# Tail of a mixture-of-experts layer: how the expert rows are read back, summed and finished

## The chip, the cores and the metric

The kernel runs on one core of one Trainium2 chip. The metric is device time in microseconds (us): the median of several executions. Beside them stands one profiled execution, whose trace is what is read below; it has its own time and its own span (first to last instruction). Engines: PE is TensorE, DVE is VectorE, ACT is ScalarE, POOL is GpSimd, SP is SyncE, which here only starts transfers and waits. A letter q behind an engine's name means its instruction queue: it waits or issues a transfer while the engine itself stays idle.

## The reference

One layer of a streaming encoder for 256 prompt tokens and 64 sample tokens of width 1024: attention of two kinds, then a mixture of experts. What the change touches is only the last line of the layer, the sum of a token's two chosen experts, its gate, and the residual:

```python
    top_w, top_i = lax.top_k(pe, TOP_K)                      # TOP_K = 2
    top_w = top_w / jnp.sum(top_w, axis=-1, keepdims=True) * pg_sel
    gate = jnp.sum(jax.nn.one_hot(eid, N_EXPERTS, dtype=jnp.float32) * top_w[..., None], axis=1)
    hid = jax.nn.silu(jnp.einsum('nd,edf->nef', hf, w1)) * jnp.einsum('nd,edf->nef', hf, w3)
    hid = hid * gate[..., None].astype(hid.dtype)
    y = jnp.einsum('nef,efd->nd', hid, w2)
    ...
    x = x + g2 * _hier_moe(h2, w_rg, b_rg, w_re, b_re, w1, w3, w2)
```

All values are fp32.

## The kernel before

Tokens lie on the 128 partitions in three tiles: tile 0 and tile 1 are the prompt (128 rows each), tile 2 is the sample (64 rows, `rows_of(2)`). Each engine has its own hand-written instruction stream; semaphores order them. Most of the time goes to attention and projections, and then to the expert loop: 16 pairs of experts, whose weights (`ew`, `e_w` in the trace) SP loads in 1 MB transfers. For each pair POOL gathers token rows, PE runs the two up projections (`hidden`) and the down projection (`down`, line 999, called through the helper `mm`, line 550), ACT and DVE bring the result into `y_sb`, weighted with the token's gate, and POOL scatters the rows with an indirect DMA (line 1881) to `y_dram` (`expert_rows` in the trace) in the chip's main memory. A token's two experts give two rows there, one in each half of the tensor, `TOK` rows apart.

After the loop comes the tail, which the change rewrites. All waits here are in program order on each engine:

- POOL waits until the last scatter has landed (`y_stored`, line 1901), and then issues six loads (line 1905), in the order tile 0, tile 2, tile 1, each time `ya` (first half of `y_dram`) and `yb` (second half). A load of a prompt tile is 512 KB, of the sample 256 KB. Each tile has its semaphore, `back[t]`, complete at 32.
- DVE takes the prompt tiles: wait for `back[t]`, `ya + yb` (line 1749), times the gate `g2b` (line 1751), plus the residual `x_sb` (line 1753), 128x1024 each, with a drain between.
- POOL takes the sample tile with the same three operations at 64x1024 (lines 1908, 1910, 1912), and then raises `y_sample_done`.
- SP stores tile 0 and tile 1 (line 530) as DVE finishes them (`y_done`), and then the sample (line 532) after `y_sample_done`; then it waits for all stores and the program ends.
- PE and ACT have nothing to do in the tail. PE's last work is a slot table (`slot_table`, names `EV` and `R`), made at the end of each round of the expert loop.

Of the kernel before, what the change touches and what calls it, by code (L numbers as in the profile page):

```python
# [7 lines left out]
P = 128  # L8
D = 1024
KD = D // P  # L10
SEQ, DEC, PAST = 256, 64, 256
TOK = SEQ + DEC
TILES = 3
# [18 lines left out]
ALU = mybir.AluOpType  # L32
# [43 lines left out]
def rows_of(t):  # L76
    return P if t < 2 else DEC


def build(nc, t_in, t_out):  # L80
    g = t_in
    ctx = ExitStack()
    with ctx:
        def sem(name):
            return ctx.enter_context(nc.semaphore(name))
# [5 lines left out]
        def place(name, shape, dt, at):  # L91
            assert at + 4 * int(np.prod(shape[1:])) <= end, name
            return nc.alloc_sbuf_tensor_at(name, shape, dt, offset=at)
# [3 lines left out]
        def take(name, shape, dt=F32):  # L97
            at = cursor[0]
            cursor[0] += (4 * int(np.prod(shape[1:])) + 31) // 32 * 32
            return place(name, shape, dt, at)  # L100

        cst = take("cst", [P, C_ALL])
        ident = cst[:, C_ID:C_ID + P]
# [28 lines left out]
        x_sb = take("x_sb", [P, TILES, D])  # L132
# [79 lines left out]
        ya, yb = (place(n, [P, TILES, D], F32, ew_at + 2 * 4 * (2 * KD * FE + 2 * D) * (j + 1)) for j, n in enumerate(("ya", "yb")))  # L212
        cursor[0] = hT_at
        g2b = take("g2b", [P, 2, D])
# [53 lines left out]
        ps = ctx.enter_context(nc.psum_tensor("ps", [P, 8, 512], F32))  # L268
# [3 lines left out]
        y_dram = nc.dram_tensor("expert_rows", [1 + 2 * TOK, D], F32).ap()  # L272
# [39 lines left out]
        g2_in = sem("g2_in")  # L312
        o_done = sem("o_done"); o_added = sem("o_added")
# [11 lines left out]
        e_y = sem("e_y"); e_ya = sem("e_ya"); e_yv = sem("e_yv")  # L325
        y_stored = [sem(f"y_stored{j}") for j in range(2)]
        back = [sem(f"back{t}") for t in range(TILES)]
        y_done = sem("y_done"); y_sample_done = sem("y_sample_done"); stored = sem("stored")


        ADA_BANK = 1
# [18 lines left out]
        def _(sp):  # L350
# [171 lines left out]
            with sp.Fori(0, count) as r:  # L522
# [2 lines left out]

                sp.wait_ge(rounds_ready, 1)
                sp.reg_load(count, rnd_i[0:1, 0:1])
            for t in range(2):
                sp.wait_ge(y_done, t + 1)
                sp.dma_start(t_out["y_prompt"][t * P:(t + 1) * P], x_sb[:, t, :]).then_inc(stored, 16)  # L530
            sp.wait_ge(y_sample_done, 1)
            sp.dma_start(t_out["y_sample"], x_sb[0:DEC, 2, :]).then_inc(stored, 16)
            sp.wait_ge(stored, 48)
            for s in a_stored + b_stored:
# [4 lines left out]
        def _(pe):  # L539
# [381 lines left out]
            def slot_table(r):  # L921

                for n in range(2):
                    built = pe.to_reg(2 * r + n + 1)
                    pe.wait_ge(r_rows, 1)
                    pe.wait_ge(r_slot, built)
                    for t in range(TILES):
                        rows = rows_of(t)
                        last = mm(ps[:, 7, 0:3 * EXPERTS], R[0:rows, 3 * n + t, :],
                                  EV[0:rows, 3 * n + t, :, :].rearrange("p a e -> p (a e)"), n == 0 and t == 0)  # L930
                    pe.free_register(built)
                last.then_inc(tab_out, 1)
# [72 lines left out]
            with pe.Fori(0, rounds) as r:  # L1005
# [8 lines left out]
                down(r, PAIRS - 1)  # L1014
                slot_table(r + 1)


        @block.scalar
        def _(act):
# [265 lines left out]
            def columns_out(r, p):  # L1285

                act.wait_ge(e_Ta, PAIRS * r + p + 1)
                act.wait_ge(e_h, PAIRS * r + p + 1)
                A(xgT[p % 2][:, 0:4, :], ps[:, 0, :].rearrange("p (k s) -> p k s", k=4), ACT.Copy).then_inc(e_xTa, 1)

            def expo(r, p):

                act.wait_ge(e_h, PAIRS * r + p + 3)
                act.wait_ge(e_hid, PAIRS * r + p + 1)
                A(h_e[p % 2][:], ps[:, 2 + p % 2, 0:FE], ACT.Exp, scale=-1.0).then_inc(e_exp, 1)  # L1295

            def hid_out(r, p):

                act.wait_ge(e_hT, PAIRS * r + p + 3)
                act.wait_ge(e_y, PAIRS * r + p + 1)  # L1300
                A(hidT[p % 2][:], ps[:, 4, 0:2 * P].rearrange("p (m s) -> p m s", m=2), ACT.Copy).then_inc(e_hTc, 1)  # L1301

            def rows_out(r, p):

                act.wait_ge(e_y, PAIRS * r + p + 3)
                act.wait_ge(y_stored[p % 2], 16 * (8 * r + p // 2 + 1))
                A(y_sb[p % 2][:, 0:512], ps[:, 5, :], ACT.Copy, scale=row_w[:, p:p + 1]).then_inc(e_ya, 1)

            with act.Fori(0, rounds) as r:
                act.wait_ge(tab_ready, r + 1)  # L1310
                columns_out(r, 0)
                for p in range(PAIRS):
                    expo(r, p)
                    if p + 1 < PAIRS:
                        columns_out(r, p + 1)
                    if p:
                        rows_out(r, p - 1)
                    hid_out(r, p)
                rows_out(r, PAIRS - 1)


        @block.vector
        def _(dve):
            V = nc.vector
# [76 lines left out]
            for k in range(KD):  # L1401
                last = V.tensor_scalar(h_sample[:, k, :], xnT[:, k, SEQ:TOK], gain1[:, k, 1:2], mod[:, k, 1:2], ALU.mult, ALU.add)
# [187 lines left out]
            for u in range(4):  # L1590
                for t in range(TILES):
                    n, r = 3 * u + t, rows_of(t)
# [56 lines left out]
            for n, eh in enumerate((eh1, eh2)):  # L1649
                dst = E1[:, n].rearrange("p t (g e) -> p t g e", g=GROUPS)  # L1650
# [71 lines left out]
            with dve.Fori(0, rounds) as r:  # L1722
# [3 lines left out]
                for half in range(2):  # L1726
                    c = slice(SLOTS * half, SLOTS * (half + 1))
                    own = ps[c, 7, 0:3 * EXPERTS].rearrange("s (a p two) -> s a p two", a=3, two=2)[:, :, :, half]
                    V.tensor_scalar(idx[c], own[:, 0:2, :], float(NO_ROW), None, ALU.add)
                    last = V.tensor_copy(row_w[c, :], own[:, 2, :])  # L1730
# [13 lines left out]


            dve.wait_ge(g2_in, 16)
            for t in range(2):
                dve.wait_ge(back[t], 32)
                V.tensor_tensor(ya[:, t, :], ya[:, t, :], yb[:, t, :], ALU.add)
                dve.drain()  # L1750
                V.tensor_tensor(ya[:, t, :], ya[:, t, :], g2b[:, 0, :], ALU.mult)
                dve.drain()
                V.tensor_tensor(x_sb[:, t, :], x_sb[:, t, :], ya[:, t, :], ALU.add).then_inc(y_done, 1)


        @block.gpsimd
        def _(pool):
            G = nc.gpsimd
# [91 lines left out]
            for n in range(2):  # L1850
                src = late_cst[:, L_ROW + 6 * n:L_ROW + 6 * n + 6].rearrange("p (t a) -> p t a", a=2)
                last = G.tensor_tensor(EV[:, 3 * n:3 * n + 3, 0:2, :], E1[:, n].unsqueeze(2).broadcast_to([P, TILES, 2, EXPERTS]),
                                       src.unsqueeze(3).broadcast_to([P, TILES, 2, EXPERTS]), ALU.mult)
# [45 lines left out]
            pool.wait_ge(setup_done, 1)  # L1899
            for j in range(2):  # L1900
                pool.wait_ge(y_stored[j], stored_rows)
            for t in (0, 2, 1):
                for n, dst in enumerate((ya, yb)):
                    first, r = 1 + n * TOK + t * P, rows_of(t)
                    pool.dma_start(dst[0:r, t, :], y_dram[first:first + r]).then_inc(back[t], 16)
            pool.wait_ge(back[2], 32)
            pool.wait_ge(g2_in, 16)
            G.tensor_tensor(ya[0:DEC, 2, :], ya[0:DEC, 2, :], yb[0:DEC, 2, :], ALU.add)
            pool.drain()
            G.tensor_tensor(ya[0:DEC, 2, :], ya[0:DEC, 2, :], g2b[0:DEC, 1, :], ALU.mult)  # L1910
            pool.drain()
            G.tensor_tensor(x_sb[0:DEC, 2, :], x_sb[0:DEC, 2, :], ya[0:DEC, 2, :], ALU.add).then_inc(y_sample_done, 1)


_SHAPES = (("y_prompt", (1, SEQ, D)), ("y_sample", (1, DEC, D)),
# [26 lines left out]
```

## Time and profile before

| | us |
|---|---|
| median of 3 runs | 851.24 (851.11 to 852.28) |
| the profiled execution, its time | 850.77 |
| the profiled execution, its span | 849.0 |
| PE busy in that span | 714.0 (84%) |
| DVE busy | 349.2 (41%) |
| POOL busy | 102.9 (12%) |

The profiled execution's time is 1.77 us longer than its span: what lies around the first and last instruction. It lies 0.47 us under the median. The profile gives shares over the whole span; the change is in its last 24 us, so what matters is read from that stretch: the chain of work that ended last, the timeline of each engine there, and the load of the DMA engines in short stretches. "Idle before" in a group of instructions names what ended the engine's wait. The column PEclk gives the TensorE clock that was granted in a stretch, as a part of 2.4 GHz; 0.50 is 1.2 GHz, and there are only these two levels.

### The profile page before, as it was taken

Reading aid. Unit: us, or ns where it says so; the run is one execution under the profiler, and the core shown is the slowest. Engines: PE = TensorE matmul, PEld = TensorE weight load, DVE = VectorE, ACT = ScalarE, POOL = GpSimd, SP = SyncE. Lnnn points to the kernel's source line nnn. Section 1 sums busy time; section 2 is a strip of 40 time slices with the busy share of each in tenths; the row PEclk is TensorE's granted clock in tenths of the full one; section 3 lists DMA queues with packets and bytes.
Section 4 is the critical chain, followed back from the end, with each engine's and each line's share of the span. In section 5 each row is a group of like instructions: output and inputs, shape, how many; then the busy total and the mean of one; then the engine's idle time right before and its main releaser. Section 6 shows DMA issues by size and latency. Waiting matters only on the chain.

```text
span 849.0 us, 13795 instructions
## 1 busy us (share of the span) xinstructions
PE 714.0 (84%) x5329; PEld 585.2 (69%) x5329; DVE 349.2 (41%) x548; ACT 271.0 (32%) x499; POOL 102.9 (12%) x161
## 2 busy tenths in 40 slices
PE   0797999999899799999988999638997887888770
PEld 0386888887699799999978999525554644644540
DVE  1556666776343243334423455531323123113123
ACT  1445455554443334455334531300111011001000
POOL 2012222222000001000100000010011001001014
PEclk9899999999899899999999999857999989989895
DMA  9947277765636576542215342699799999999705
GB/s 323 326 137 225 70 210 219 217 196 181 199 101 187 148 224 178 135 114 77 80 49 178 101 148 100 252 422 416 320 416 417 418 419 417 419 416 418 313 17 182
DMA packets 131176, 199.17 MB, mean 235 GB/s; under 512 B 11688, under 2 KB 113464, under 8 KB 117816
## 3 DMA queue, kind: packets, MB, share of 16 engines
q1 hardware_dynamic: 123032, 185.63, 61.7%
q0 software_dynamic: 6208, 11.02, 3.7%
q10 hardware_dynamic: 1888, 1.86, 0.7%
q8 instruction: 32, 0.52, 0.3%
q14 instruction: 16, 0.13, 0.0%
HBM read 193.47 MB, written 16.55 MB: 247 GB/s over the span
## 4 chain that ended last, share of the span: by engine, by line
PE 63%; issue 20%; ACT 6%; DVE 4%; POOL 2%; POOLq 2%; ACTq 1%; DVEq 1%; DMA 0%
PE ps L550 35%; PE ps L545 8%; PE ps L547 7%; PE ps L546 7%; ACT w_hi L1066 3%; DVE w_lo L1378 1%; PE ps L945 1%; PE ps L949 1%; PE ps L981 1%; PE ps L713 1%; ACT sig_r L1183 1%; DVEq L1587 1%; ACT z_na L1228 1%; PE ps L696 0%; POOLq L1777 0%
## 5 line engine op out<-in xcount | busy, mean ns | idle before, releaser
L550 PE MATMUL ps<-e_w,xgT 128*64 128x256 f32 x1024 | 129.7, 417 | 32.6 <-issue 31.3
L550 PEld LDWEIGHTS ps<-e_w,xgT 128*64 128x64 f32 x1024 | 91.2, 151 | 66.8 <-issue 40.2
L545 PE MATMUL ps<-hT_hi,w_hi 128*128 128x320 f32 x320 | 102.6, 321 | 5.5 <-DVE w_lo L1378 5.2
L1378 DVE TENSOR_TENSOR w_lo<-raw,w_hi 128x2048 fp32r<-128x2048 f32 (+1 forms) x27 | 71.5, 2647 | 83.9 <-ACT w_hi L1066 83.9
L546 PE MATMUL ps<-hT_lo,w_hi 128*128 128x320 f32 x320 | 99.9, 312 | 0.0
L547 PE MATMUL ps<-hT_hi,w_lo 128*128 128x320 f32 x320 | 99.8, 312 | 0.0
L1707 DVE TENSOR_SCALAR h_s<-h_e 128x256 f32<-128x256 f32 x16 | 4.7, 294 | 162.8 <-ACT h_e L1295 162.8
L1066 ACT ACTIVATE w_hi<-raw 128x2048 fp32r<-128x2048 f32 (+1 forms) x27 | 59.1, 2190 | 28.3 <-PE ps L547 28.3
L545 PEld LDWEIGHTS ps<-hT_hi,w_hi 128*128 128x128 f32 x320 | 61.0, 191 | 7.9 <-DVE w_lo L1378 5.5
L546 PEld LDWEIGHTS ps<-hT_lo,w_hi 128*128 128x128 f32 x320 | 61.2, 191 | 0.0
L547 PEld LDWEIGHTS ps<-hT_hi,w_lo 128*128 128x128 f32 x320 | 61.1, 191 | 0.0
L550 PE MATMUL ps<-e_w,hidT 128*64 128x512 f32 x256 | 58.4, 598 | 0.6 <-ACT hidT L1301 0.6
L1295 ACT ACTIVATE h_e<-ps 128x256 f32<-128x256 f32 x16 | 6.2, 384 | 153.5 <-PE ps L550 153.5
L545 PE MATMUL ps<-w_hi,hT_hi 128*128 128x384 f32 x128 | 45.3, 354 | 0.0
L546 PE MATMUL ps<-w_lo,hT_hi 128*128 128x384 f32 x128 | 43.5, 340 | 0.0
L547 PE MATMUL ps<-w_hi,hT_lo 128*128 128x384 f32 x128 | 43.4, 339 | 0.0
L1881 POOL DMA_INDIRECT expert_rows<-y_sb,idx x16 | 16.2, 1012 | 215.4 <-DVE y_sb L1720 189.5
L545 PE MATMUL ps<-oT_hi,w_hi 128*128 128x320 f32 x128 | 40.5, 316 | 1.1 <-DVE oT_lo L1545 1.1
L546 PE MATMUL ps<-oT_lo,w_hi 128*128 128x320 f32 x128 | 40.2, 314 | 0.0
L547 PE MATMUL ps<-oT_hi,w_lo 128*128 128x320 f32 x128 | 40.2, 314 | 0.0
L550 PEld LDWEIGHTS ps<-e_w,hidT 128*64 128x64 f32 x256 | 17.5, 136 | 29.6 <-issue 27.8
L550 PE MATMUL ps<-ada_late,c_cols 128*32 128x128 f32 x512 | 32.7, 283 | 0.0
(261 smaller groups left out, 1283.8 us busy)
## 6 DMA issues: line engine op xcount, KB each, us to landing
e_w<-in_w SPq DMA_DIRECT2D x96, 1024.0 KB, 23.3
raw<-in_w_in SPq DMA_DIRECT2D x45, 512.0 KB
ada_late<-in_w_ada SPq DMA_DIRECT2D x16, 1024.0 KB, 5.1
ada_first<-in_w_ada SPq DMA_DIRECT2D x8, 1024.0 KB, 21.7
raw<-in_w_in SPq DMA_DIRECT2D x8, 1024.0 KB
raw<-in_w_oa SPq DMA_DIRECT2D x4, 1024.0 KB
raw<-in_w_ob SPq DMA_DIRECT2D x4, 1024.0 KB
raw<-in_w_out SPq DMA_DIRECT2D x4, 1024.0 KB
```

The costliest lines, as they stand in the source:

```text
L545: nc.tensor.matmul(out, lhs_hi, rhs_hi, start=first, stop=False, skip_group_check=True)
L546: nc.tensor.matmul(out, lhs_hi, rhs_lo, start=False, stop=False, skip_group_check=True)
L547: return nc.tensor.matmul(out, lhs_lo, rhs_hi, start=False, stop=last, skip_group_check=True)
L550: return nc.tensor.matmul(out, lhs, rhs, start=first, stop=last, skip_group_check=True)
L713: last = nc.tensor.transpose(ps[:, b, c * P:(c + 1) * P], amap[:, n * P:(n + 1) * P], ident)
L945: last = nc.tensor.transpose(ps[:, 0, k * P:(k + 1) * P], xg[p % RING][:, k:D:KD], ident)
L949: last = nc.tensor.transpose(ps[:, 1, (k - 4) * P:(k - 3) * P], xg[p % RING][:, k:D:KD], ident)
L981: last = nc.tensor.transpose(ps[:, 4, m * P:(m + 1) * P], hid[j][:, m:FE:2], ident)
L1066: A(w_hi[j][:, :, 0:width], raw[j][:, :, 0:width], ACT.Copy).then_inc(split_hi, 1)
L1183: A(sig_r[m][:], sig[m][:], ACT.Ln, bias=1.0)
L1378: V.tensor_tensor(w_lo[j][:, :, 0:width], raw[j][:, :, 0:width], f32(w_hi[j][:, :, 0:width]), ALU.subtract).then_inc(split_done, 1)
L1881: G.indirect_dma_start(y_dram, bass.IndirectOffsetOnAxis(ap=idx[:, 1, p:p + 1], axis=0), y_sb[j][:], None, bounds_check=2 * TOK, oob_is_er ...
```

## The change

Three things change, all behind the expert loop.

1. Loads. POOL, when the last scatter has landed, raises a new semaphore `scattered`. SP then loads both rows of tile 0, ACT both rows of tile 1, POOL itself both rows of tile 2. The six transfers and their bytes are the same.
2. Sum. For each tile in the order 0, 1, 2 PE waits for `back[t]` and adds the two rows: for each half of 512 columns one matmul with the identity as the stationary operand and `ya` as the moving one, and one with `yb` that accumulates on it, into PSUM banks `2t` and `2t + 1`. That is 4 fp32 matmuls of 512 columns a tile, 12 in all.
3. Finish. DVE finishes all three tiles with two operations each: PSUM times `g2b` into `ya`, and `x_sb + ya`. POOL's three operations on the sample are gone. SP stores tile 0 and the sample, ACT stores tile 1.

```diff
+            sp.wait_ge(scattered, 1)
+            for n, dst in enumerate((ya, yb)):
+                sp.dma_start(dst[:, 0, :], y_dram[1 + n * TOK:1 + n * TOK + P]).then_inc(back[0], 16)
+            sp.wait_ge(y_done, 1)
+            sp.dma_start(t_out["y_prompt"][0:P], x_sb[:, 0, :]).then_inc(stored, 16)
+            sp.wait_ge(y_done, 3)
             sp.dma_start(t_out["y_sample"], x_sb[0:DEC, 2, :]).then_inc(stored, 16)
...
+            for t in range(TILES):
+                rows = rows_of(t)
+                pe.wait_ge(back[t], 32)
+                for half in range(2):
+                    c = slice(half * 512, (half + 1) * 512)
+                    mm(ps[0:rows, 2 * t + half, :], ident[0:rows, 0:rows], ya[0:rows, t, c], True, False)
+                    last = mm(ps[0:rows, 2 * t + half, :], ident[0:rows, 0:rows], yb[0:rows, t, c], False)
+                last.then_inc(o_done, 1)
...
+            act.wait_ge(scattered, 1)
+            for n, dst in enumerate((ya, yb)):
+                act.dma_start(dst[:, 1, :], y_dram[1 + n * TOK + P:1 + n * TOK + 2 * P]).then_inc(back[1], 16)
+            act.wait_ge(y_done, 2)
+            act.dma_start(t_out["y_prompt"][P:2 * P], x_sb[:, 1, :]).then_inc(stored, 16)
...
-            for t in range(2):
-                dve.wait_ge(back[t], 32)
-                V.tensor_tensor(ya[:, t, :], ya[:, t, :], yb[:, t, :], ALU.add)
+            for t in range(TILES):
+                rows = rows_of(t)
+                dve.wait_ge(o_done, 13 + t)
+                V.tensor_tensor(ya[0:rows, t, :].rearrange("p (b c) -> p b c", b=2), ps[0:rows, 2 * t:2 * t + 2, :],
+                                g2b[0:rows, t // 2, :].rearrange("p (b c) -> p b c", b=2), ALU.mult)
                 dve.drain()
-                V.tensor_tensor(ya[:, t, :], ya[:, t, :], g2b[:, 0, :], ALU.mult)
-                dve.drain()
-                V.tensor_tensor(x_sb[:, t, :], x_sb[:, t, :], ya[:, t, :], ALU.add).then_inc(y_done, 1)
+                V.tensor_tensor(x_sb[0:rows, t, :], x_sb[0:rows, t, :], ya[0:rows, t, :], ALU.add).then_inc(y_done, 1)
...
-            for t in (0, 2, 1):
-                for n, dst in enumerate((ya, yb)):
-                    first, r = 1 + n * TOK + t * P, rows_of(t)
-                    pool.dma_start(dst[0:r, t, :], y_dram[first:first + r]).then_inc(back[t], 16)
-            pool.wait_ge(back[2], 32)
-            pool.wait_ge(g2_in, 16)
-            G.tensor_tensor(ya[0:DEC, 2, :], ya[0:DEC, 2, :], yb[0:DEC, 2, :], ALU.add)
...
+            pool.nop().then_inc(scattered, 1)
+            for n, dst in enumerate((ya, yb)):
+                first = 1 + n * TOK + 2 * P
+                pool.dma_start(dst[0:DEC, 2, :], y_dram[first:first + DEC]).then_inc(back[2], 16)
```

On POOL, behind the last scatter, these rows stand in the kernel before (`ya` and `yb` are the two row buffers, a row with 64x1024 is the sample's; in brackets the semaphores that an instruction waits for):

```order
L1905 DMA ya<-expert_rows 128x1024 [waits y_stored1,y_stored0,setup_done]
L1905 DMA yb<-expert_rows 128x1024
L1905 DMA ya<-expert_rows 64x1024
L1905 DMA yb<-expert_rows 64x1024
L1905 DMA ya<-expert_rows 128x1024
L1905 DMA yb<-expert_rows 128x1024
L1908 TENSOR_TENSOR ya<-ya,yb 64x1024 [waits g2_in,back2]
L1910 TENSOR_TENSOR ya<-ya,g2b 64x1024
L1912 TENSOR_TENSOR x_sb<-x_sb,ya 64x1024
```

and these in the changed one, from the last scatter to the end:

```order
L1898 DMA expert_rows<-y_sb_180,idx 641x1024 [waits e_yv,y_stored0,e_ya,setup_done]
L1903 REGISTER_ALU
L1903 COMPARE_AND_BRANCH
L1915 ISA
L1922 DMA ya<-expert_rows 64x1024 [waits y_stored1,setup_done,y_stored0]
L1922 DMA yb<-expert_rows 64x1024
```

Four of POOL's six loads have moved to SP and ACT, and its three operations are gone.

On PE the program before ends with the slot table of the round behind the last:

```order
L924 ISA
L550 MATMUL ps<-EV,R 128x96 [waits r_slot,r_rows]
L550 MATMUL ps<-EV,R 128x96 x2
L924 REGISTER_ALU
L550 MATMUL ps<-EV,R 128x96 [waits r_slot,r_rows]
L550 MATMUL ps<-EV,R 128x96 x2
L1005 REGISTER_ALU
L1005 COMPARE_AND_BRANCH
```

In the changed one the sums stand behind the loop's branch (`cst` holds the identity). The rows of tile 1 follow those of tile 0 in the same form, the sample's with 64x512:

```order
L552 MATMUL ps<-EV,R 128x96 x2
L1007 REGISTER_ALU
L1007 COMPARE_AND_BRANCH
L552 MATMUL ps<-ya,cst 128x512 [waits back0]
L552 MATMUL ps<-yb,cst 128x512
L552 MATMUL ps<-ya,cst 128x512
L552 MATMUL ps<-yb,cst 128x512
L552 MATMUL ps<-ya,cst 128x512 [waits back1]
```

PE now stands between the loads and DVE, tile after tile.

## Rows read from the trace of the kernel before

**Rows 1.** Page, chain that ended last: shares of the span by engine.
```profile
PE 63%; issue 20%; ACT 6%; DVE 4%; POOL 2%; POOLq 2%; ACTq 1%; DVEq 1%; DMA 0%
```

**Rows 2.** Chain in order of time, its end: start us, us, what.
```profile
822.78 2.72 DMA expert_rows<-y_sb,idx
...
826.07 0.58 POOL ya L1905
...
829.33 4.84 issue
834.16 3.15 POOLq L1909
837.31 3.26 issue
840.57 2.62 POOLq L1911
...
843.32 2.36 POOLq L83
```

**Rows 3.** Timeline of the tail: start us, us, engine, line, operation, idle before.
```profile
831.29 1.23 DVE L1749 TENSOR_TENSOR ya<-ya,yb 128x1024 f32<-128x1024 f32 x1 [8.26 <-DMA yb<-expert_rows]
832.60 1.23 DVE L1751 TENSOR_TENSOR ya<-ya,g2b 128x1024 f32<-128x1024 f32 x1
...
835.15 6.22 SPq L530 DMA_DIRECT2D out_y_prompt<-x_sb  x2
836.68 1.72 DVE L1749 TENSOR_TENSOR ya<-ya,yb 128x1024 f32<-128x1024 f32 x1 [1.55 <-DMA yb<-expert_rows]
...
845.71 0.52 SPq L532 DMA_DIRECT2D out_y_sample<-x_sb  x1
```

**Rows 4.** Half-microsecond stretches: busy us by engine, then PEclk, DMA share, GB/s.
```profile
825.00:825.50 0.50, 0.00 (x0) 0.00 (x0) 0.00 (x0) 0.00 (x0) 0.00 (x0) 0.50 0.05 8
827.00:827.50 0.50, 0.00 (x0) 0.00 (x0) 0.00 (x0) 0.00 (x0) 0.50 (x2) 0.50 0.53 74
828.00:828.50 0.50, 0.00 (x0) 0.00 (x0) 0.00 (x0) 0.00 (x0) 0.50 (x2) 0.50 1.04 319
830.00:830.50 0.50, 0.00 (x0) 0.00 (x0) 0.00 (x0) 0.00 (x0) 0.00 (x0) 0.50 0.96 393
...
832.50:833.00 0.50, 0.00 (x0) 0.00 (x0) 0.42 (x2) 0.00 (x0) 0.00 (x0) 0.50 1.13 221
...
835.00:835.50 0.50, 0.00 (x0) 0.00 (x0) 0.12 (x1) 0.00 (x0) 0.50 (x1) 0.50 1.09 434
835.50:836.00 0.50, 0.00 (x0) 0.00 (x0) 0.00 (x0) 0.00 (x0) 0.50 (x1) 0.50 0.20 74
```

**Rows 5.** The scatters of line 1881, sixteen of 512 KB: issue to landing.
```profile
DMA to landing us min/median/max: 2.6/8.1/9.2
```

**Rows 6.** Page, DMA issues: the weight loads that run beside them.
```profile
e_w<-in_w SPq DMA_DIRECT2D x96, 1024.0 KB, 23.3
```

**Rows 7.** Timeline of the last down projection; DVE reads PSUM before and behind it.
```profile
815.29 0.42 DVE L1711 TENSOR_TENSOR h_s<-h_s,ps 128x256 f32<-128x256 f32 x1
...
817.41 3.65 PE L550 MATMUL ps<-e_w,hidT 128*64 128x512 f32 x16 [0.63 <-ACT hidT L1301]
...
821.10 0.75 DVE L1720 TENSOR_SCALAR y_sb<-ps,row_w 128x512 f32<-128x512 f32 x1 [4.14 <-PE ps L550]
```

**Rows 8.** Timeline of PE in attention: an fp32 matmul on the whole array.
```profile
315.82 0.86 PE L550 MATMUL ps<-z_sp,cst 128*128 128x384 f32 x2
316.52 0.38 PE L550 MATMUL ps<-z_sp,ones_neg 128*128 128x128 f32 x2
```

**Rows 9.** Stretches behind a restart of PE: columns as in the stretches above.
```profile
689.23:694.98 5.75, 5.75 (x28) 3.66 (x30) 0.00 (x0) 0.00 (x0) 0.00 (x0) 0.50 1.01 417
...
803.83:807.62 3.79, 3.79 (x20) 2.74 (x22) 0.00 (x0) 0.00 (x0) 0.00 (x0) 0.55 0.28 109
807.62:811.41 3.79, 3.79 (x38) 3.02 (x37) 0.00 (x0) 0.00 (x0) 0.00 (x0) 1.00 0.02 8
```

More of the change, by code:

```diff
@@ L327, in build @@
         back = [sem(f"back{t}") for t in range(TILES)]
-        y_done = sem("y_done"); y_sample_done = sem("y_sample_done"); stored = sem("stored")
+        y_done = sem("y_done"); scattered = sem("scattered"); stored = sem("stored")
         ADA_BANK = 1
@@ L527, in _ @@
                 sp.reg_load(count, rnd_i[0:1, 0:1])
-            for t in range(2):
-                sp.wait_ge(y_done, t + 1)
-                sp.dma_start(t_out["y_prompt"][t * P:(t + 1) * P], x_sb[:, t, :]).then_inc(stored, 16)
-            sp.wait_ge(y_sample_done, 1)
+            sp.wait_ge(scattered, 1)
[4 more added lines that the diff above has]
+            sp.wait_ge(y_done, 3)
             sp.dma_start(t_out["y_sample"], x_sb[0:DEC, 2, :]).then_inc(stored, 16)
@@ L1746, in _ @@
             dve.wait_ge(g2_in, 16)
-            for t in range(2):
-                dve.wait_ge(back[t], 32)
-                V.tensor_tensor(ya[:, t, :], ya[:, t, :], yb[:, t, :], ALU.add)
+            for t in range(TILES):
[3 more added lines that the diff above has]
+                                g2b[0:rows, t // 2, :].rearrange("p (b c) -> p b c", b=2), ALU.mult)
                 dve.drain()
-                V.tensor_tensor(ya[:, t, :], ya[:, t, :], g2b[:, 0, :], ALU.mult)
-                dve.drain()
-                V.tensor_tensor(x_sb[:, t, :], x_sb[:, t, :], ya[:, t, :], ALU.add).then_inc(y_done, 1)
+                V.tensor_tensor(x_sb[0:rows, t, :], x_sb[0:rows, t, :], ya[0:rows, t, :], ALU.add).then_inc(y_done, 1)
         @block.gpsimd
@@ L1901, in _ @@
                 pool.wait_ge(y_stored[j], stored_rows)
-            for t in (0, 2, 1):
-                for n, dst in enumerate((ya, yb)):
-                    first, r = 1 + n * TOK + t * P, rows_of(t)
-                    pool.dma_start(dst[0:r, t, :], y_dram[first:first + r]).then_inc(back[t], 16)
-            pool.wait_ge(back[2], 32)
-            pool.wait_ge(g2_in, 16)
-            G.tensor_tensor(ya[0:DEC, 2, :], ya[0:DEC, 2, :], yb[0:DEC, 2, :], ALU.add)
[L1909 to L1912, printed above, removed]
+            pool.nop().then_inc(scattered, 1)
+            for n, dst in enumerate((ya, yb)):
+                first = 1 + n * TOK + 2 * P
+                pool.dma_start(dst[0:DEC, 2, :], y_dram[first:first + DEC]).then_inc(back[2], 16)
 _SHAPES = (("y_prompt", (1, SEQ, D)), ("y_sample", (1, DEC, D)),
```

## The prediction

> **What bounds the kernel now.** First the page's chain that ended last: PE holds 63% of it [rows 1], so over the whole span the matmuls are the bound. The change touches none of that; it lies in the last 24 us, and there the chain looks different. Read it in order of time [rows 2]: the last scatter, issued at 822.78, lands 2.72 us later, at 825.50; POOL begins to issue its six loads at 826.07 and is through at 829.33; then it waits 4.84 us for the sample's rows; and from 834.16 on the chain is POOL's own three operations, 3.15, 2.62 and 2.36 us, with a hole of 3.26 us between the first two. They end at 845.68, and SP stores the sample at 845.71 [rows 3]. The span ends at 849.0, so this store and the end of the program take 3.3 us. DVE is not on that path: it has the rows of tile 0 at 831.29 and of tile 1 at 836.68 [rows 3].
>
> The second view is the load of the DMA engines [rows 4]. Packets of the six loads run from about 827.1 to 835.5. They fill the engines from 828.0 on (share near 1.0), at 319 to 434 GB/s for prompt tiles and only 221 GB/s while the 64-row sample is moved. So the loads are bound by the DMA engines, not by their issue, except for the first microsecond.
>
> The third view is the column PEclk: PE has stopped before 825 and its clock stands at 0.50, which is 1.2 GHz, through the whole tail [rows 4].
>
> So now the path is: scatter landed (825.5), sample's rows there (834.2), POOL's 11.5 us, store 3.3 us.
>
> **The change, part by part.**
>
> *POOL's sample work goes.* 834.16 to 845.68, 11.5 us, leaves the path. What is late next is PE, which must sum three tiles, and DVE behind it.
>
> *The loads start on three queues.* SP and ACT need no software issue of 0.55 us each. SP's store issued at 835.15 [rows 3] had packets before 836.0 [rows 4], at most 0.85 us later; POOL's first load took about 1.0 us (826.07 to 827.1), and POOL waited 0.57 us behind the landing before that. With SP released at about 825.65, packets begin at 826.5, 0.6 us earlier than now. When does tile 0 land, call it T0? Earliest: SP's tile is served alone, as POOL's first is now: 831.29 - 0.6 = 830.7. Latest: all share evenly and end as the last load does now: 836.68 - 0.6 = 836.1. Between them: SP's and ACT's tiles together are 2.1 MB, 5.2 us at some 400 GB/s, from 826.5 to 831.7, and landing is seen about 0.8 us behind the last packet (830.5 and 831.29 for tile 0): 832.5. The sample takes up to 2.4 us of the engines in between (half a megabyte at 221 GB/s): 834.9. I take the middle, T0 = 833.7, because queues share here and none goes first: scatters that POOL issued beside a weight queue 23.3 us deep [rows 6] landed after 8.1 us in the median and 2.6 at best [rows 5]. They neither waited for that queue nor passed it.
>
> The Trainium skill, page "DMA: Bandwidth & Descriptors", section "Issuing engines are not separate DMA queues", speaks against this part: transfers from scalar, sync or gpsimd run on the same 16 DMA engines and interleave, and several issuers save only the issue time. By that rule, too, this part gains the 0.6 us alone; if instead each queue had its own bandwidth, T0 would be near 830.7. The full DMA share behind a single queue agrees with the rule [rows 4]; no row here shows two hardware queues side by side.
>
> *PE's 12 matmuls.* An fp32 matmul shows as two records, that is two passes: the last down projection has 8 in its code and 16 in the trace [rows 7]. Those work in two halves of the array side by side (128*64), so each half passes 8 times 512 columns in 3.65 us, 0.456 us a pass. Nearest check on the whole array: two passes of 384 columns before the next instruction starts, 315.82 to 316.52, 0.70 us [rows 8], which scales to 0.47 for 512 columns. A tile here is 4 matmuls, 8 passes: 3.65 us at full clock, the sample too, since its columns count and not its 64 rows. Three tiles: 10.9 us (11.2 by the second row). Lower bound: if the halves were not side by side, a pass would be 3.65/16 = 0.228 us, and three tiles 5.5 us.
>
> *The clock.* PE starts at half clock after 9 us of idling. Behind seven waits of 3 to 4 us in the expert loop the full clock came back 3.8 to 5.75 us after PE's restart; the longest and the shortest stand in [rows 9], with 0.50 and 0.55 granted until then. 20 records fitted in 3.79 us, and 38 in the next 3.79 us at 1.00. Half of such a stretch is lost: 1.9 to 2.9 us. I take 2.3. Upper bound: the clock never rises, then the whole 10.9 us come once more.
>
> *DVE.* Two operations a tile instead of three. The second is an SBUF add like those of 1.23 us; the first reads PSUM. 0.42 us for 256 columns and 0.75 for 512 [rows 7] bound it between 1.23 and 1.5 us. With the pitch of 1.31 us between two operations (831.29 to 832.60), 1.31 + 1.23 = 2.6 us a tile with the handover (DVE's 821.10 follows PE's end at 821.06). That is less than PE's 3.65, so tiles 0 and 1 hide under PE's next tile, and only the sample's 2.6 us are on the path. If PE were twice as fast this cover would go, and DVE's 3 x 2.6 would be the bound (below).
>
> *What costs nothing.* The nop for `scattered` is POOL's and SP, ACT and POOL wait anyway; SP and ACT have nothing queued behind their waits but the stores. The stores of tiles 0 and 1 leave while PE works on later tiles. Only the sample's store stays, at 3.3 us as now.
>
> *Sum.* 833.7 + 10.9 + 2.3 + 2.6 + 3.3 = 852.8, against a span of 849.0: **3.8 us longer**. POOL's 11.5 us are replaced by 10.9 + 2.3 + 2.6 = 15.8, and the start is 0.5 us earlier. The profiled execution took 850.77 with its 1.77 us around the span, so it would be 854.6; it lies 0.47 under the median of 851.24, so the median becomes 855.0. With all lower bounds of this case (T0 832.5, clock 1.9) it is 853.4, with the upper ones (T0 836.1, passes 11.2, clock 2.9, DVE 0.3 more) 858.6.
>
> **The rivals.**
>
> *SP first.* Tile 0 lands at 830.7, and PE sums it while the others arrive. The rest is as above, as tile 1 is there by 836.1, before PE asks for it at half clock. 3.0 us less: span 849.8, median 852.0, no measurable change. For it: SP issues first by a hair. Against it: the sharing in rows 5. Chance 0.12.
>
> *Cheap passes* (the other side). If a pass of 512 columns costs 0.228 us, tile 0 is summed at half clock in 3.65 us and then DVE is the bound, three times 2.6: T0 + 3.65 + 7.8 + 3.3. That is 848.5 with T0 = 833.7 (median 850.7, no change) and 845.5 with 830.7 (median 847.7, faster). It decides where T0 lies under 832.5. Against it: 0.70 us for two passes of 384 columns on the whole array [rows 8]. The same holds if the identity matmul were done in one pass. Chance 0.06, faster 0.04 and unchanged 0.02 of it.
>
> *Cold to the end.* The clock stays at 0.50 for all 12 matmuls: 10.9 us in place of 2.3, span 861.4, median 863.6. Against it: in the expert loop it came back within 5.75 us of steady work [rows 9]. The Trainium skill, page "TensorE: Matmul & The Clock Gate", section "HAM oscillation — how this bites in real kernels", warns of small bursts between waits for DMA that run throttled; the granted 0.50 behind earlier waits agrees. It would decide if PE had to wait between tiles, and it does not, if they land together. Chance 0.06.
>
> **How the numbers follow.** My forecast, 855.0, has 0.72; SP first 0.12, cheap passes 0.06, cold 0.06; 0.04 is left for something slower that I don't see. A measurement of this kernel tells about 0.2% from no change, 1.7 us: under 849.5 is faster, over 852.9 slower. So faster 0.04, same 0.15 (SP first, cheap passes, and 0.01 of the forecast's own edge), slower 0.81. The range runs from 851.6, which takes in SP first, to 858.6, the forecast's upper end; cold and cheap passes are left out.
>
> **What would show it.** In the changed kernel's trace: (1) first packets of the loads near 826.5 and `back[0]` seen by PE between 832.5 and 835; (2) 24 records on PE, the first ones 0.85 to 0.95 us apart at clock 0.50, later ones 0.43 to 0.47; PE done about 13 us after its start; (3) DVE waiting for PE before each tile; (4) POOL empty behind its two loads; (5) the last store issued near 849.5. The forecast is wrong if PE starts under 831, if passes come at 0.23 us, or if DVE or a late load, not PE, holds the end.

## The result, and the profile after

The changed kernel is slower. In 8 runs beside 8 of the kernel before it took 854.59 us in the median (853.48 to 856.96) against 850.46; the ratio is 1.0072, with a 95% interval of 1.005 to 1.0094, so about 6 us of 850 (4.3 to 8.0); the two medians lie 4.1 us apart. The prediction had named 855.0 and a range of 851.6 to 858.6. The profiled execution took 854.27 us with a span of 852.5; before it was 849.0.

The part ahead of the tail is the same work in both kernels, but it varies a little from run to run: the last scatter landed at 825.50 in the trace before and at 824.48 in this one. So from here on a kernel is judged by its **tail**: the time from the landing of the last scatter to the end of the span. Before it is 849.0 - 825.50 = 23.5 us, after 852.5 - 824.48 = 28.0. The change costs 4.5 us of tail, inside the interval of the timed runs.

The chain that ended last, in order of time (start us, us, what):

```profile
821.76 2.72 DMA expert_rows<-y_sb,idx
...
825.02 9.38 DMA yb<-expert_rows
834.40 0.04 issue
834.44 12.16 PE ps L552 x24
...
846.62 1.22 DVE ya L1767
...
847.92 1.22 DVE x_sb L1770
```

Set beside [rows 2], POOL's steps are gone. In their place stand one load that takes 9.38 us, 12.16 us of PE in 24 records, and two operations of DVE. The timeline of the tail (start us, us, engine, line, operation, idle before):

```profile
824.63 0.33 SPq L530 DMA_DIRECT2D ya<-expert_rows  x1
824.64 0.36 ACTq L1334 DMA_DIRECT2D ya<-expert_rows  x1
...
825.14 0.58 POOL L1922 DMA_DIRECT2D ya<-expert_rows  x1 [2.28 <-DMA expert_rows<-y_sb,idx]
...
834.44 2.07 PE L552 MATMUL ps<-ya,cst 128*128 128x512 f32 x2 [10.70 <-DMA yb<-expert_rows]
836.30 1.56 PE L552 MATMUL ps<-yb,cst 128*128 128x512 f32 x2
837.70 1.02 PE L552 MATMUL ps<-ya,cst 128*128 128x512 f32 x2
838.56 1.02 PE L552 MATMUL ps<-yb,cst 128*128 128x512 f32 x2
...
839.69 1.23 DVE L1767 TENSOR_TENSOR ya<-ps,g2b 128x1024 f32<-128x1024 f32 x1 [17.67 <-PE ps L552]
...
846.62 1.22 DVE L1767 TENSOR_TENSOR ya<-ps,g2b 64x1024 f32<-64x1024 f32 x1 [1.05 <-PE ps L552]
847.92 1.22 DVE L1770 TENSOR_TENSOR x_sb<-x_sb,ya 64x1024 f32<-64x1024 f32 x1
849.16 0.52 SPq L534 DMA_DIRECT2D out_y_sample<-x_sb  x1
```

The loads do go out earlier: SP issues 0.15 us behind the landing (824.63 - 824.48), POOL did 0.57 us behind it (826.07 - 825.50). But PE has its first tile 9.96 us behind the landing, where DVE had it 5.79 us behind before (831.29 in [rows 3]). Each transfer's issue to landing shows why (line: output, queue, kind, count, size, us to landing):

```profile
ya<-expert_rows SPq DMA_DIRECT2D x1, 512.0 KB, 4.8
ya<-expert_rows ACTq DMA_DIRECT2D x1, 512.0 KB, 5.0
yb<-expert_rows SPq DMA_DIRECT2D x1, 512.0 KB, 9.4
yb<-expert_rows ACTq DMA_DIRECT2D x1, 512.0 KB, 9.9
ya<-expert_rows POOLq DMA_DIRECT2D x1, 256.0 KB, 8.0
yb<-expert_rows POOLq DMA_DIRECT2D x1, 256.0 KB, 9.5
```

SP's and ACT's transfers go in step, and the second row of every tile lands within a microsecond of the others: nothing is there early, so nothing can be worked on early. Half-microsecond stretches of that time (busy us by engine, then PEclk, DMA share, GB/s), to be set beside [rows 4]:

```profile
826.50:827.00 0.50, 0.00 (x0) 0.00 (x0) 0.00 (x0) 0.00 (x0) 0.00 (x0) 0.50 0.88 270
828.00:828.50 0.50, 0.00 (x0) 0.00 (x0) 0.00 (x0) 0.00 (x0) 0.00 (x0) 0.50 1.01 418
831.00:831.50 0.50, 0.00 (x0) 0.00 (x0) 0.00 (x0) 0.00 (x0) 0.00 (x0) 0.50 0.99 279
833.50:834.00 0.50, 0.00 (x0) 0.00 (x0) 0.00 (x0) 0.00 (x0) 0.00 (x0) 0.50 0.77 197
837.50:838.00 0.50, 0.50 (x2) 0.19 (x1) 0.00 (x0) 0.00 (x0) 0.00 (x0) 1.00 0.00 0
```

The DMA engines are full from 827 to 833.5, at first at 418 GB/s and from 830 on at some 270 GB/s, between the rate of prompt tiles and that of the 64-row sample (221 in [rows 4]). The last row shows PE's clock: it was back at 1.00 at 837.4, 2.9 us after PE's start.

### The profile page after: what moved, and what is told of

It reads as the page before. It is cut to its first block, busy times and chain, and to the rows that moved or that the text cites. A ratio compares the mean times of both kernels' runs of the same rounds, so it can differ in the third digit from the quotient of the medians.

```text
span 852.5 us, 13837 instructions
## 1 busy us (share of the span) xinstructions
PE 724.8 (85%) x5353; PEld 588.9 (69%) x5353; DVE 348.8 (41%) x548; ACT 271.5 (32%) x499; POOL 92.6 (11%) x154
## 4 chain that ended last, share of the span: by engine, by line
PE 63%; issue 19%; ACT 6%; DVE 5%; POOL 2%; DMA 1%; DVEq 1%; ACTq 1%; POOLq 1%; SPq 0%
PE ps L552 36%; PE ps L547 8%; PE ps L549 7%; PE ps L548 7%; ACT w_hi L1077 3%; DVE w_lo L1395 1%; PE ps L947 1%; DMA yb<-expert_rows 1%; PE ps L951 1%; PE ps L983 1%; PE ps L715 1%; ACT sig_r L1194 1%; DVEq L1604 1%; ACT z_na L1239 0%; PE ps L698 0%
```

## The experiments

Two reasons could be read from the traces. **Theory:** the loss has two parts. Three queues make all tiles land together, some 10 us behind the scatter, and PE's sum is longer than the work of DVE that it saves. **Rivals:** the sharing of the queues is all of it and PE's sum is free where it has something to hide under; or PE is all of it; or PE's clock.

Each ratio below is taken to runs of the kernel before that were made beside the experiment. Their median was 848.51 us beside the first four experiments and 848.37 us beside the last three, against 850.46 us beside the changed kernel, so kernels of different sets are compared by their ratios and tails, not by their times.

### The three queues alone

Loads as in the changed kernel, sums and finish as before (behind its two loads POOL does the sample's three operations again, and PE does nothing):

```diff
-            for t in range(TILES):
-                rows = rows_of(t)
-                pe.wait_ge(back[t], 32)
...
+            pool.wait_ge(back[2], 32)
+            pool.wait_ge(g2_in, 16)
+            G.tensor_tensor(ya[0:DEC, 2, :], ya[0:DEC, 2, :], yb[0:DEC, 2, :], ALU.add)
```

> Part 1 alone: the six loads go out on SP, ACT and POOL as in the changed kernel, the sums and the finish stay on DVE and POOL as before. Call tail the time from the landing of the last scatter to the end of the span: 23.5 us before, 28.0 us in the changed kernel. Theory (all tiles land together about 10 us behind the scatter, and PE's 12.2 us are the larger part of the loss): POOL's sample chain of 11.5 us starts at 10 and not at 8.7, DVE's prompt tiles at 10: tail 24.8 to 26.5, 1.3 to 3 us longer than before. Rival A (sharing three queues is the whole loss): tail 28. Rival B (each queue brings bandwidth of its own): tail under 23.5.

Measured: 854.26 us in the median, ratio 1.0053 (1.003 to 1.0076). In its profile the last scatter landed at 826.35 (823.63 + 2.72) and the span was 853.6: tail 27.25, 3.75 us longer than before and above what I had expected. The timeline of the tail:

```profile
836.07 1.23 DVE L1758 TENSOR_TENSOR ya<-ya,yb 128x1024 f32<-128x1024 f32 x1 [12.19 <-DMA yb<-expert_rows]
837.12 2.37 POOL L1917 TENSOR_TENSOR ya<-ya,yb 64x1024 f32<-64x1024 f32 x1 [8.96 <-DMA yb<-expert_rows]
837.38 3.20 DVE L1760 TENSOR_TENSOR ya<-ya,g2b 128x1024 f32<-128x1024 f32 x1
...
841.79 1.22 DVE L1758 TENSOR_TENSOR ya<-ya,yb 128x1024 f32<-128x1024 f32 x1
...
842.45 2.75 POOL L1919 TENSOR_TENSOR ya<-ya,g2b 64x1024 f32<-64x1024 f32 x1 [2.96 <-issue]
843.08 3.20 DVE L1760 TENSOR_TENSOR ya<-ya,g2b 128x1024 f32<-128x1024 f32 x1
845.36 3.12 POOL L1921 TENSOR_TENSOR x_sb<-x_sb,ya 64x1024 f32<-64x1024 f32 x1 [0.15 <-issue]
846.36 3.20 DVE L1762 TENSOR_TENSOR x_sb<-x_sb,ya 128x1024 f32<-128x1024 f32 x1
848.50 0.52 SPq L534 DMA_DIRECT2D out_y_sample<-x_sb  x1
849.60 0.35 ACTq L1328 DMA_DIRECT2D out_y_prompt<-x_sb  x1
```

DVE has its first tile 9.72 us behind the landing and POOL the sample at 10.77: the landing part of the theory holds. What I had missed is what happens then. Because all tiles come at once, DVE and POOL now work side by side for the whole time, and three of DVE's six operations take 3.20 us where they take 1.23 alone: 5.9 us of waiting. DVE, not POOL, ends last, and behind it the end takes 4.0 us (849.60 to 853.6) and not 3.3, as two stores now go out close together. So late landing, this collision and the end together cost 3.75 us; no run separates them. Rival B (under 23.5) falls. Rival A (28) does not fall by this run, whose 27.25 us are nearer to it than to my range; it falls by the next one, where the sum on PE costs 2.8 us with the loads as before.

The Trainium skill, page "SBUF — State Buffer", section "SBUF: two separate sides", says that DVE with two SBUF inputs and a GpSimd operation exclude each other for the whole instruction. The trace agrees: the 3.20 us operation that starts at 837.38 ends at 840.58, 1.09 us behind the end of POOL's at 839.49, so it waited and ran mostly behind it. The other two end 1.08 us behind POOL's operations.

POOL waits in the same way, and in the kernel before too, which the prediction did not see. These rows stand in its tail:

```profile
833.90 1.23 DVE L1753 TENSOR_TENSOR x_sb<-x_sb,ya 128x1024 f32<-128x1024 f32 x1
834.21 3.11 POOL L1908 TENSOR_TENSOR ya<-ya,yb 64x1024 f32<-64x1024 f32 x1 [4.88 <-DMA yb<-expert_rows]
...
839.78 1.23 DVE L1753 TENSOR_TENSOR x_sb<-x_sb,ya 128x1024 f32<-128x1024 f32 x1
840.59 2.60 POOL L1910 TENSOR_TENSOR ya<-ya,g2b 64x1024 f32<-64x1024 f32 x1 [3.28 <-issue]
843.35 2.33 POOL L1912 TENSOR_TENSOR x_sb<-x_sb,ya 64x1024 f32<-64x1024 f32 x1 [0.15 <-issue]
```

POOL's third operation meets no work of DVE and takes 2.33 us. The two before it, and the three in the run with the queues alone, start while DVE is in an operation, and each of the five ends 2.18 to 2.20 us behind the end of that operation (833.90 + 1.23 = 835.13, POOL's end 837.32). The hole of 3.28 us, 3.26 in [rows 2], spans two operations of DVE on tile 1 (838.48 to 841.01). So of POOL's 11.5 us some 4.2 were waiting for DVE: an estimate, 11.5 less three times 2.33 and two handovers of 0.15.

### The sum on PE alone

Loads on POOL as before, sums and finish as in the changed kernel, all stores on SP:

```diff
-            act.wait_ge(scattered, 1)
-            for n, dst in enumerate((ya, yb)):
-                act.dma_start(dst[:, 1, :], y_dram[1 + n * TOK + P:1 + n * TOK + 2 * P]).then_inc(back[1], 16)
...
+            for t in (0, 2, 1):
+                for n, dst in enumerate((ya, yb)):
+                    first, r = 1 + n * TOK + t * P, rows_of(t)
+                    pool.dma_start(dst[0:r, t, :], y_dram[first:first + r]).then_inc(back[t], 16)
```

> Parts 2 and 3 alone: POOL issues all six loads as before, in the order tile 0, sample, tile 1; PE sums and DVE finishes as in the changed kernel; SP stores. Theory: tile 0 lands 5.8 us behind the scatter, PE takes 12.2 us from there because the other tiles land under its work, then 2.6 for DVE and 3.3 for the store: tail 23.9, about 0.4 us longer than before (23.5), 4 us shorter than the changed kernel. Rival A (the sum on PE costs nothing where loads are not shared): tail 20 to 21. Rival C (PE is the loss wherever it stands): tail 27 to 28.

Measured: 851.88 us, ratio 1.0032 (1.0011 to 1.0052). Scatter landed at 825.08, span 851.4: tail 26.3, 2.8 us longer than before, where I had expected 0.4. Rival A falls (20 to 21). Rival C (27 to 28) is missed by 0.7 us only, less than the clock's spread below; what refutes it is the next run, where PE sums and the tail is 23.9. The theory's mechanism stands, but two of its numbers were too good. Two stretches of this run, PE's sum cut where its clock changed (columns as above):

```profile
831.73:838.30 6.57, 6.57 (x8) 2.72 (x9) 0.00 (x0) 0.00 (x0) 0.00 (x0) 0.53 0.70 183
838.30:845.50 7.20, 7.17 (x17) 2.32 (x15) 4.90 (x4) 0.00 (x0) 0.00 (x0) 1.00 0.20 83
```

Here the full clock came back only 6.1 us after PE's start, not 2.9 as in the changed kernel, so the sum took 13.8 us and not 12.2. And PE began 6.65 us behind the landing, where DVE had tile 0 at 5.8 to 6.0 with the same loads; this last 0.7 us lies in the load: from the issue of tile 0's second row to its first use it was 5.5 us here (826.22 to 831.73) and 4.65 before (826.64 to 831.29). Why stays open.

### One hardware queue

The changed kernel with all loads on SP, tile after tile:

```diff
             sp.wait_ge(scattered, 1)
-            for n, dst in enumerate((ya, yb)):
-                sp.dma_start(dst[:, 0, :], y_dram[1 + n * TOK:1 + n * TOK + P]).then_inc(back[0], 16)
+            for t in range(TILES):
+                for n, dst in enumerate((ya, yb)):
+                    first, r = 1 + n * TOK + t * P, rows_of(t)
+                    sp.dma_start(dst[0:r, t, :], y_dram[first:first + r]).then_inc(back[t], 16)
```

> The changed kernel with all six loads on SP, in the order tile 0, tile 1, sample; SP makes all stores. Theory: on one queue tile 0 lands first, 4.5 to 5 us behind the scatter, PE works under the other loads: tail 5 + 12.5 + 2.6 + 3.3 = 23.4, 4.6 us shorter than the changed kernel. Rival (the DMA engines finish all tiles late whatever the queue): T0 near 10, tail 28.

Measured: 850.37 us, ratio 1.0014 (0.999 to 1.0039). Scatter landed at 828.33, span 852.2: tail 23.9, expected 23.4.

```profile
833.21 2.07 PE L555 MATMUL ps<-ya,cst 128*128 128x512 f32 x2 [5.62 <-DMA yb<-expert_rows]
...
848.91 0.50 SPq L537 DMA_DIRECT2D out_y_sample<-x_sb  x1
```

PE starts 4.88 us behind the landing, 5.1 us earlier than with three queues. It loses 1.0 of that because the clock came back later (4.9 us after the start), and the tail is 4.1 us shorter than in the changed kernel. The rival (28) falls. The transfers and their bytes are the same; what differs is that they stand in one queue, in the order of use. A run with three queues and the order of use kept would part the two; there is none. The low rate has moved too: the sample's loads are now the last, and the slow stretch is at the end (columns as above), where in the kernel before, with the sample second, it was in the middle [rows 4]:

```profile
834.00:834.50 0.50, 0.50 (x2) 0.27 (x1) 0.00 (x0) 0.00 (x0) 0.00 (x0) 0.50 1.04 426
836.00:836.50 0.50, 0.50 (x2) 0.27 (x1) 0.00 (x0) 0.00 (x0) 0.00 (x0) 0.50 1.12 180
```

The Trainium skill, page "DMA: Bandwidth & Descriptors", section "Issuing engines are not separate DMA queues", states that issuing from several engines saves only the issue time. These two runs agree: the last of the six loads landed 10.7 us behind the scatter with three queues and 11.0 with one. They also show that it can cost much more than it saves: 5.1 us of the first landing.

### No PE at all

All loads on SP in the same order, and DVE alone sums and finishes each of the three tiles:

```diff
+            for t in (0, 1, 2):
+                rows = rows_of(t)
+                dve.wait_ge(back[t], 32)
+                V.tensor_tensor(ya[0:rows, t, :], ya[0:rows, t, :], yb[0:rows, t, :], ALU.add)
+                dve.drain()
+                V.tensor_tensor(ya[0:rows, t, :], ya[0:rows, t, :], g2b[0:rows, t // 2, :], ALU.mult)
+                dve.drain()
+                V.tensor_tensor(x_sb[0:rows, t, :], x_sb[0:rows, t, :], ya[0:rows, t, :], ALU.add).then_inc(y_done, 1)
```

> All six loads on SP, in the order tile 0, tile 1, sample; DVE alone sums and finishes all three tiles with three operations each; neither PE nor POOL computes in the tail. Theory: three tiles of 3.9 us on DVE from 4.5 to 5 us on, then the store: 5 + 11.7 + 3.3 = 20.0, 3.5 us shorter than before and 8 us shorter than the changed kernel. Rival (loads bound the tail): 10 us for the last tile, 3.9, 3.3 = 17.2. Rival (PE's sum is worth its place, since it takes a third of DVE's work): tail over that of the same loads with PE, 23.4.

Measured: 846.35 us, ratio 0.9958 (0.9937 to 0.998): faster than both kernels. Scatter landed at 826.99, span 846.9: tail 19.9, expected 20.0.

```profile
832.23 1.23 DVE L1758 TENSOR_TENSOR ya<-ya,yb 128x1024 f32<-128x1024 f32 x1 [7.70 <-DMA yb<-expert_rows]
833.54 1.23 DVE L1760 TENSOR_TENSOR ya<-ya,g2b 128x1024 f32<-128x1024 f32 x1
...
835.98 1.22 DVE L1758 TENSOR_TENSOR ya<-ya,yb 128x1024 f32<-128x1024 f32 x1
...
843.53 0.50 SPq L538 DMA_DIRECT2D out_y_sample<-x_sb  x1
```

From the first tile on DVE never waits; a tile takes 3.75 us (832.23 to 835.98). Both rivals fall (17.2, and over 23.4). Against the run before it, with the same loads, that is 4.0 us less, in the tails and in the medians (850.37 and 846.35, beside the same runs of the kernel before): this is what the sum on PE costs.

### The kernel before, with the sample on DVE

Loads on POOL as before; POOL's three operations move to DVE, in the order tile 0, sample, tile 1:

```diff
-            for t in range(2):
+            for t in (0, 2, 1):
+                rows = rows_of(t)
                 dve.wait_ge(back[t], 32)
...
-            pool.wait_ge(back[2], 32)
-            pool.wait_ge(g2_in, 16)
```

> The kernel before with one edit: the sample's three operations move from POOL to DVE, in the order tile 0, sample, tile 1; loads stay on POOL in that order. Theory: DVE runs three tiles of 3.9 us without a hole from 5.8 us on, tile 1 is stored last: 5.8 + 11.7 + 3.3 = 20.8, 2.7 us shorter than before. Rival (DVE cannot keep up, the sample's 3.9 us come on top of DVE's end of 841.0 in the trace of before): 841.0 + 3.9 + 3.1 - 825.5 = 22.5.

Measured: 845.44 us, ratio 0.9967 (0.9936 to 0.9998). Scatter landed at 826.33, span 846.6: tail 20.3, 3.2 us shorter than before; expected 20.8, and the rival (22.5) falls. The timed runs put the gain at 0.2 to 5.4 us.

```profile
832.29 1.23 DVE L1753 TENSOR_TENSOR ya<-ya,yb 128x1024 f32<-128x1024 f32 x1 [8.43 <-DMA yb<-expert_rows]
...
843.60 0.35 SPq L533 DMA_DIRECT2D out_y_prompt<-x_sb  x1
```

All nine operations of DVE take 1.21 to 1.23 us here, as POOL computes nothing. Of the improvement over the kernel before, nearly all is POOL's compute; moving the loads from POOL to SP adds 0.4 us in the traces, which the timed runs cannot tell apart.

### A warm PE

The changed kernel with nine idle matmuls ahead of the first sum, so that the clock has risen:

```diff
+            for w in range(9):
+                mm(ps[:, 7, :], ident, x_sb[:, w % 2, 0:512], True)
+
             for t in range(TILES):
                 rows = rows_of(t)
                 pe.wait_ge(back[t], 32)
```

> The changed kernel with 9 more fp32 matmuls of 512 columns on PE between the expert loop and the first sum; they read x_sb, write a bank that nothing reads any more, and take 7.7 us at full clock, so they end before tile 0 lands. Only PE's clock at the start of the sums changes. Theory: the 24 passes take 10.3 us at 0.429 each and not 12.2, everything behind PE moves with it: tail 26.1 to 26.5 against 28.0. Rival (the clock is not on the path): tail 28.0.

Measured: 853.65 us, ratio 1.005 (1.0019 to 1.0081). Scatter landed at 824.62, span 851.4: tail 26.8.

```profile
824.36 10.74 PE L552 MATMUL ps<-x_sb,cst 128*128 128x512 f32 x18
...
834.93 1.02 PE L552 MATMUL ps<-ya,cst 128*128 128x512 f32 x2
```

PE's sum went at 1.00 all through and took 10.6 us (834.93 to 845.57) instead of 12.2. The idle matmuls themselves ran at half clock at first, took 10.74 us and not the 7.7 I had counted, and so pushed the start to 10.3 us behind the landing. The tail is 1.2 us shorter: 1.5 gained in the sum, 0.3 lost at its start. The rival (28.0) falls in the trace: the clock is on the path, and 1.5 us is less than either of the other two parts, 4.1 for the queues and 4.0 for PE. The timed runs do not tell this kernel from the changed one: the intervals of their ratios overlap (1.0019 to 1.0081 and 1.005 to 1.0094).

### One row per token

> The changed kernel without the matmuls that read yb: the second expert's row is loaded but left out of the sum. PE has 12 passes and not 24. Theory: PE needs 3.4 us a tile at half clock and 1.7 at full, so DVE with 2.6 us a tile becomes the bound behind the first tile: 10 + 3.4 + 7.8 + 3.3 = 24.5, 3.5 us shorter than the changed kernel. If PE alone were the bound the tail would be 6 us shorter; if the loads alone, as long as now.

Measured with one profiled run, 851.18 us: scatter landed at 825.33, span 849.4, tail 24.1 (expected 24.5).

```profile
835.05 7.12 PE L552 MATMUL ps<-ya,cst 128*128 128x512 f32 x12 [10.45 <-DMA yb<-expert_rows]
838.70 1.23 DVE L1766 TENSOR_TENSOR ya<-ps,g2b 128x1024 f32<-128x1024 f32 x1 [15.84 <-PE ps L552]
...
841.15 1.22 DVE L1766 TENSOR_TENSOR ya<-ps,g2b 128x1024 f32<-128x1024 f32 x1
```

With half the passes PE is done in 7.1 us, DVE no longer waits between tiles (pitch 2.45 us), and the tail is 3.9 us shorter. So the price per pass sets the end of the changed kernel, as the sum had it, until DVE becomes the bound.

## Why the prediction was right, point by point

All tails in one table (us):

| kernel | loads | sum and finish | first tile behind the landing | tail |
|---|---|---|---|---|
| before | POOL, 0-2-1 | DVE, sample on POOL | 5.8 | 23.5 |
| changed | SP, ACT, POOL | PE and DVE | 10.0 | 28.0 |
| queues alone | SP, ACT, POOL | DVE, sample on POOL | 9.7 | 27.25 |
| PE sum alone | POOL, 0-2-1 | PE and DVE | 6.65 | 26.3 |
| one queue | SP, 0-1-2 | PE and DVE | 4.9 | 23.9 |
| no PE, SP | SP, 0-1-2 | DVE | 5.2 | 19.9 |
| no PE, POOL | POOL, 0-2-1 | DVE | 6.0 | 20.3 |

- **The new bound.** That PE takes POOL's place on the path, with one DVE finish and the sample's store behind it, is what the chain shows. The run without PE bears it out: 4.0 us less with the same loads.
- **T0.** The step put it at 833.7 with the scatter landing at 825.5, so 8.2 us behind; it was 9.96, near the upper end of the bounds (10.6). The mechanism chosen (queues share, none goes first) was right. The size was off by 1.8 us because I took the middle of two ways to count, though the reason given, that queues share, spoke for the later (834.9, so 9.4). Tile 0's second row waits for nearly all bytes, the slow sample's among them: by 833.5 the engines had moved some 2.5 of the 2.6 MB, and PE saw the tile at 834.44. The start of the packets, 1.0 us behind the landing, came out as counted (825.5 here), but from a row that was misread: the bytes of all stretches up to 836.0, of which [rows 4] shows some, add up to the six loads' 2.6 MB, so the packets before 836.0 were the last load's, and SP's store had its first ones at 836.0. SP first (0.12) is refuted by the six landings, and one queue shows what it would have been worth.
- **Passes.** 24 records, as counted. At full clock the start-to-start pitch is 0.43 us (837.70 to 838.56 for two), against 0.456 from [rows 7]: 10.3 us and not 10.9. Cheap passes at 0.228 are refuted.
- **The clock.** It cost 1.9 us by the count of passes (12.2 - 10.3) and 1.5 by the warm run (12.2 - 10.6), against 2.3 in the sum; cold to the end did not happen. The other runs show 2.9 to 6.1 us until the full clock was back, so this term differs from run to run by some 1.6 us.
- **DVE and the store.** 2.54 us from 846.62 to 849.16, against 2.6; PSUM cost nothing over SBUF (1.23 against the bound of 1.5). Store and end 3.3 us, as before.
- **The sum.** Against the landing it was to be 852.8 - 825.5 = 27.3, and it was 28.0: T0 1.8 too early, PE 1.0 too long. That the median came within 0.4 us of the forecast is in part luck: these two errors oppose each other, the scatter landed 1.0 us earlier in this trace than in the one before, and the 851.24 us from which the forecast was counted became 850.46 with 8 runs.
- **What I did not price.** The effects of the two halves do not add: queues alone 3.75, sum alone 2.8, together 4.5. Two things in the traces speak to that, and no run takes them apart: the collision of DVE and POOL, which is in the run with the queues alone and which the sum on PE removes with POOL's work, and the late clock of the run with the sum alone (1.6 us). The prediction took POOL's 11.5 us as one block with DVE off the path; some 4.2 us of it were waits for DVE (above), so by this count DVE was not off it. It also did not ask what DVE would do with the sample. That would have been the better change: 3.2 us gained in the traces. DVE alone behind three queues was not run; by this table it would end near 9.7 + 3 x 3.75 + 3.3 = 24.2 (an estimate). Taken out one after the other, the three queues (4.1) and PE's sum (4.0) weigh the same, so PE was not the larger part, as my first expectation had it.

## What to carry to other kernels

Spreading the loads of one stage over three queues made them land together here; when the first piece can be worked on alone, put all on one queue in the order of use. Adding two fp32 tiles of 128x1024 by matmuls with the identity takes 8 passes, 3.4 us at full clock, and saves one vector operation of 1.23 us; in this tail it also started at half clock: 12.2 us of PE stand against the 3.7 us that DVE would need for the three sums. Before work is taken from a slow helper engine by a new one, count what the nearest engine would need if it did all of it.

## What the runs showed of the hardware that was not expected

- The time until TensorE has its full clock again after a long rest is not one number: 2.9 us after the restart in the changed kernel, 3.2 with one row per token, 4.9 with one queue, 5.6 in the warm run and 6.1 with the sum alone, all with the same kind of work (fp32 passes of 512 columns, back to back). PE had rested 5.6 to 10.7 us in four of them. In the warm run it had hardly rested: the idle matmuls followed the slot table, during which the clock had fallen (at 823.1).
- Two rows of 512 KB on SP and two on ACT advance in step: first rows landed at 4.8 and 5.0 us, second rows at 9.4 and 9.9.
- A DVE operation of 1.23 us showed as 3.20 us when POOL was at work on SBUF tiles, three times in one run, and a POOL operation of 2.33 us as up to 3.12: the wait for the other engine is counted as busy time. A longer wait of POOL showed as idle time before it (3.28 us in the kernel before, where DVE was at work).
